# Delta rule of a two-block network: the triangular inverse transposed by VectorE in squares of 32

## The chip, the cores and the metric

The kernel runs on one core of a Trainium2 chip. The metric is the device time of one execution in microseconds (us); the time of the kernel before is the median of three runs.

## What is computed

The reference is a forward pass over 512 tokens of width 1024 (and 256 context tokens): a first block (dilated attention, a recurrent layer, a mixture of experts), and a second one of two layers (an even layer with attention and gated linear attention, an odd layer with a short convolution and a gated delta rule, each with an MLP). All of it is float32. The change touches the delta rule of the odd layer alone:

```python
def gdn_chunked(q, k, v, log_a, beta, s0):      # chunks of C = 64 tokens, 8 heads
    ...
    decay = jnp.where(incl, jnp.exp(jnp.where(incl, diff, 0.0)), 0.0)
    kb = k * beta
    a_mat = jnp.where(strict, jnp.einsum('bhnid,bhnjd->bhnij', kb, k) * decay, 0.0) + jnp.eye(C, dtype=F32)
    rhs = jnp.concatenate([v * beta, kb * jnp.exp(g)[..., None]], axis=-1)
    sol = lax.linalg.triangular_solve(a_mat, rhs, left_side=True, lower=True)
    ...
```

For every chunk and head a unit triangular matrix of 64x64 has to be inverted. It runs forwards and backwards over 768 tokens, which are 12 chunks.

## The kernel before

`delta` (line 3322) does the delta rule in a pipeline of STEPS = 12 problems. Problem `u` is one chunk forwards and one backwards (index z), for 8 heads each (the 8 heads lie as two halves of the 128 partitions, index g, and four columns of 64): sixteen matrices of 64x64, a tile of 128x512. Buffers and PSUM regions are there twice, for even and odd `u`.

The inverse is made by doubling. N is the strict triangle; six masks `lev[:, l]` (LEVELS = 6) cut out of it the blocks that join two finished blocks of 2^l to one of 2^(l+1). N0 is level 0. After level l the inverse so far is block-diagonal with blocks of 2^(l+1). It is kept transposed, in `Tt`. Level by level, from l = 1 to 5:

- `product(u, l)` (3458), TensorE: sixteen matmuls of 64x64x64, masked N times `Tt`, into PSUM region 0; then eight transposes of `Tt` through the identity (line 3471) into region 1.
- `take(u, l)` (3623), ScalarE: waits for both, copies region 0 to M and region 1 to T (lines 3627, 3628).
- `update(u, l)` (3474), TensorE: waits for both copies; sixteen matmuls T times M into region 0.
- `inverse(u, l)` (3744), VectorE: `Tt` minus region 0, into `Tt` (line 3753). For l = 5 also `Tb`, `Tt` times beta (line 3758).

Level 0 is `first(u)` (3449): sixteen matmuls of N0 with the identity, which is a transpose, and `inverse(u, 0)`, identity minus that, into `Tt` (line 3748). N itself comes from `sums`, `spread` and `keys` on TensorE, `differences` (3706) and `matrix` (3715: EB at line 3719, N at 3725, N0 at 3731) on VectorE, and `decays` (3630) with `eg` (3640) on ScalarE. The masked N of levels 1 to 5 are made by GpSimd in `level(u, l)` (3839, each operation has line 3824).

Each float32 matmul here is two instructions. A matmul reads one half of the partitions (rows 0 to 63 or 64 to 127) and writes one half of PSUM's partitions; which halves these are is in `rows(..., g)` and in the last argument of `piece`. `product` before reads half g and writes half z, bank g; `update` reads half z and writes half g, bank z.

The order of each engine's queue is written by hand, in a loop over n = 0 to 13 in which problem `new` = n goes through levels 0 to 2, `old` = n - 1 through levels 3 to 5 and `s` = n - 2 through the state recurrence (`values`, `minus`, `gain`, `from_state`, `outputs` on TensorE, `half` on VectorE and ScalarE, `fade` on ScalarE, `advance` and `collect` on VectorE). One pass of this loop is called a beat below. From u = 4 on (`lat`) a problem has outputs, and `spread`, `queries` and `scores` belong to it. TensorE's order in a beat is: product(old,3), sums, values, update(old,3), minus, keys, spread, product(old,4), first(new), gain, update(old,4), product(new,1), product(old,5), update(new,1), from_state, update(old,5), outputs, product(new,2), queries, weigh, update(new,2). VectorE's: differences, inverse(old,3), half, matrix(new), inverse(new,0), inverse(old,4), advance, inverse(new,1), inverse(old,5), collect, inverse(new,2), scores(old). ScalarE's: take(old,3), decays, half, take(old,4), fade, take(new,1), take(old,5), take(new,2), weights. `sums` waits for `scores` of the problem before the one before, which frees its PSUM region.

In the profile most matmuls have line 3408 (a helper) and are known by their tiles. The tiles N, N0, Tt, T, M and Tb lie in rooms that the profile calls gdn_raw and mlp_ring.

## Time and profile before

| | us |
|---|---|
| median of 3 runs | 2944.53 (2937.66 to 2946.17) |
| profiled execution | 2938.93 |
| span of its instructions | 2937.1 |
| mean granted TensorE clock | 0.965 |
| TensorE busy in the span | 2732.4 (93%) |
| VectorE busy | 1145.6 (39%) |
| ScalarE busy | 933.3 (32%) |
| GpSimd busy | 407.8 (14%) |

The table is over the whole network, of which the stage of the delta rule is a tenth: it starts with `sums` at 2215.74 us and gives its last outputs at about 2500 us. So the shares of the table say little about it, and the rows below are of this stage. Engines are PE (TensorE matmul), PEld (its weight loads), DVE (VectorE), ACT (ScalarE), POOL (GpSimd). In a timeline consecutive instructions of one form are merged: the first number is the start of the first, the second the time to the end of the last, and a bracket tells how long the engine had been idle and what released it.

### The profile page before, as it was taken

What the parts mean: (1) busy time and instruction counts of PE and PEld (TensorE: products, weight loads), DVE (VectorE), ACT (ScalarE), POOL (GpSimd) and SP (SyncE); (2) the same over time, 40 slices, a digit from 0 to 9 for tenths busy, and PEclk for the clock granted to TensorE, in tenths of its full rate; (3) what the DMA queues carried; (4) which work ended last, traced back from release to release, by engine and by line L of the source; (5) the groups of instructions that cost most, each with busy time, mean ns of one, the idle gap of its engine ahead of it and who ended that gap; (6) DMA issues with size and microseconds to landing.
All of it is one profiled execution on the core that took longest, in us unless ns stands there. A gap on an engine that the chain in (4) does not pass through costs nothing. (4 is left out here: it accounts for less than half of the span.)

```text
span 2937.1 us, 50199 instructions
## 1 busy us (share of the span) xinstructions
PE 2732.4 (93%) x21562; PEld 2054.4 (70%) x21562; DVE 1145.6 (39%) x1644; ACT 933.3 (32%) x1534; POOL 407.8 (14%) x334
## 2 busy tenths in 40 slices
PE   8988889999999899899999999998996788799998
PEld 6764654444444785666788888886785777688887
DVE  3225342322333416644432333323444454544333
ACT  4235331111112224355331221213474545432222
POOL 0005120000000402343100000010004564100001
PEclk9999889999999999999999999999998899899999
DMA  6537718999995212000112112111210000222331
GB/s 248 201 127 278 291 58 355 401 404 405 404 397 209 71 55 60 23 30 30 57 58 72 57 60 69 57 57 61 86 36 31 4 4 28 91 86 88 99 100 57
DMA packets 160240, 389.56 MB, mean 133 GB/s; under 512 B 16719, under 2 KB 107754, under 8 KB 147274
## 3 DMA queue, kind: packets, MB, share of 16 engines
q1 hardware_dynamic: 147834, 198.40, 20.0%
q10 hardware_dynamic: 12240, 188.75, 15.8%
q8 instruction: 129, 2.11, 0.3%
q14 instruction: 37, 0.30, 0.0%
HBM read 381.36 MB, written 5.77 MB: 132 GB/s over the span
## 5 line engine op out<-in xcount | busy, mean ns | idle before, releaser
L2143 PE MATMUL ps<-mlp_h_low,mlp_w_high 128*128 128x512 f32 (+1 forms) x768 | 272.0, 354 | 0.0
L2143 PE MATMUL ps<-mlp_h_high,mlp_w_high 128*128 128x512 f32 (+1 forms) x768 | 271.9, 354 | 0.0
L2143 PE MATMUL ps<-mlp_h_high,mlp_w_low 128*128 128x512 f32 (+1 forms) x768 | 271.6, 354 | 0.0
L1997 ACT ACTIVATE mlp_w_high<-mlp_ring 128x2048 fp32r<-128x2048 f32 x64 | 122.2, 1912 | 316.2 <-PE ps L2143 316.2
L2143 PE MATMUL ps<-mlp_x_low,mlp_w_high 128*128 128x512 f32 (+1 forms) x576 | 204.0, 354 | 0.0
L2143 PE MATMUL ps<-mlp_x_high,mlp_w_high 128*128 128x512 f32 (+1 forms) x576 | 203.9, 354 | 0.0
L2143 PE MATMUL ps<-mlp_x_high,mlp_w_low 128*128 128x512 f32 (+1 forms) x576 | 203.7, 354 | 0.0
L254 POOL TENSOR_TENSOR aT<-aT 128x512 f32<-128x512 f32 (+1 forms) x30 | 59.6, 1986 | 1031.1 <-ACT aT L246 1030.6
L2001 DVE TENSOR_TENSOR mlp_w_low<-mlp_ring,mlp_w_high 128x2048 fp32r<-128x2048 f32 x64 | 146.6, 2293 | 62.4 <-ACT mlp_w_high L1997 62.4
L2207 DVE SCALAR_TENSOR_TENSOR hT<-ps,mod,hT 128x512 f32<-128x512 f32 x96 | 63.5, 662 | 256.0 <-PE ps L2143 256.0
L2143 PEld LDWEIGHTS ps<-mlp_h_high,mlp_w_high 128*128 128x128 f32 x768 | 145.3, 189 | 20.4
L2143 PEld LDWEIGHTS ps<-mlp_h_high,mlp_w_low 128*128 128x128 f32 x768 | 145.1, 189 | 20.2
L2143 PEld LDWEIGHTS ps<-mlp_h_low,mlp_w_high 128*128 128x128 f32 x768 | 145.2, 189 | 20.0
L1863 DVE TENSOR_TENSOR hT<-hT,ps 128x512 f32<-128x512 f32 x128 | 79.4, 683 | 181.6 <-PE ps L1699 181.6
L2196 DVE TENSOR_TENSOR mlp_square<-mlp_relu 128x768 f32<-128x768 f32 (+1 forms) x64 | 52.8, 826 | 249.2 <-ACT mlp_relu L2165 248.8
L2165 ACT ACTIVATE mlp_relu<-ps 128x512 f32<-128x512 f32 x96 | 49.7, 527 | 296.2 <-PE ps L2143 218.4
L3171 PE MATMUL ps<-odd_x_high,conv_w_parts 128*128 128x512 f32 (+1 forms) x448 | 121.3, 358 | 3.1 <-DVE conv_w_parts L3269 3.1
L2143 PEld LDWEIGHTS ps<-mlp_x_high,mlp_w_high 128*128 128x128 f32 x576 | 108.9, 189 | 15.2
L2143 PEld LDWEIGHTS ps<-mlp_x_high,mlp_w_low 128*128 128x128 f32 x576 | 108.9, 189 | 15.3
L2143 PEld LDWEIGHTS ps<-mlp_x_low,mlp_w_high 128*128 128x128 f32 x576 | 108.9, 189 | 15.0
L1704 PE MATMUL ps<-e_wu,aT 128*64 128x512 f32 x512 | 116.9, 598 | 0.0
L1704 PE MATMUL ps<-e_wg,aT 128*64 128x512 f32 x512 | 116.2, 595 | 0.7 <-ACT aT L1784 0.7
(557 smaller groups left out, 5922.8 us busy)
## 6 DMA issues: line engine op xcount, KB each, us to landing
mlp_ring<-in_mlp_w_dram SPq DMA_DIRECT2D x64, 1024.0 KB, 5.3
e_wg<-in_w_gate_dram ACTq DMA_DIRECT2D x15, 4096.0 KB, 14.9
e_wu<-in_w_up_dram ACTq DMA_DIRECT2D x15, 4096.0 KB, 14.6
ring<-in_w_down_dram ACTq DMA_DIRECT2D x15, 4096.0 KB, 14.1
ring<-in_ada_w_dram SPq DMA_DIRECT2D x16, 2048.0 KB, 8.8
h_rest<-in_ada_w_dram SPq DMA_DIRECT2D x8, 2048.0 KB, 8.4
ring<-in_w_in_dram SPq DMA_DIRECT2D x6, 2048.0 KB, 11.1
proj_ring<-in_even_w_in_dram SPq DMA_DIRECT2D x8, 1024.0 KB, 5.0
```

Of the source, the lines that this page charges most:

```text
L254: pool.tensor_tensor(total, self.square_of(self.E, 0, self.T) if n == 1 else total, self.square_of(self.E, n, self.T), ALU.add)\
L1704: last = pe.matmul(E.ps[SLOTS * s:SLOTS * (s + 1), bank * BANK:(bank + 1) * BANK], xg[:, par, k, half * P + s * SLOTS:half * P + (s + 1) * ...
L1863: dve.tensor_tensor(E.hT[:, n, 0:S], E.hT[:, n, 0:S], E.bank(4 + n % 4), ALU.add).then_inc(added, 1)
L1997: act.activation(self.high[:, slot], self.ring[:, slot], ACT.Copy).then_inc(self.w_high, 1)
L2001: dve.tensor_tensor(self.low[:, slot], self.ring[:, slot], self.high[:, slot].bitcast(FP), ALU.subtract).then_inc(self.w_low, 1)
L2143: last = pe.matmul(bank(st, n, s, b - a), w[:, st % 2, k, n * P:(n + 1) * P], x[:, k, a:b], start=(k == 0 and p == 0), stop=(k == KT - 1 a ...
L2165: act.activation(r[:, n, a:b], bank(st, n, s, b - a), ACT.Relu).then_inc(relus, 1)
L2196: dve.tensor_tensor(sq[:, n, :], r[:, n, :], r[:, n, :], ALU.mult).then_inc(squares, 1)
L2207: dve.scalar_tensor_tensor(out=E.hT[:, k, a:b], in0=bank(st, n, s, b - a), scalar=E.mod[:, layer, 40 + k, s:s + 1], in1=E.hT[:, k, a:b], o ...
L3171: last = pe.matmul(E.bank(2 * (n % 3) + half, b - a), wp[:, part, n % 2, kk, :], xp[:, kk, a:b], start=(kk == 0 and i == 0), stop=(kk == K ...
```

## The change

- `product` loses its eight transposes. It reads half g and now writes half g, bank z.
- `update` reads half g and writes half g. T now has the layout of `Tt`, M the layout that the new `product` writes (`zi`).
- T is made by VectorE: `dve.transpose` turns every square of 32x32 of a 128x512 tile in its place, from SBUF to SBUF. The inverse so far has blocks of 32 at most where a T is needed, so this is its transpose. It stands right behind the subtraction of `inverse(u, l)` for l = 1 to 4.
- `first` is gone from TensorE. `inverse(u, 0)` subtracts N0 from the identity in SBUF, which gives T, and a transpose of it gives `Tt`.
- `take` copies M alone.
- `level(u, 3)` on GpSimd waits for the new T of level 0 in place of `first`.

Two names of semaphores that are no longer used are left out here:

```diff
--- before.py
+++ after.py
@@ -3352,6 +3352,7 @@
         azj = lambda t: t.rearrange("p (a z j n) -> p a z j n", a=2, z=2, j=2)
 
         iz = lambda t: t.rearrange("p (i z n) -> p z i n", i=4, z=2)
+        zi = lambda t: t.rearrange("p (z i n) -> p z i n", z=2, i=4)
         blocks = lambda t: t.rearrange("p (m n) -> p m n", n=64)
 
         def region(u, r):
@@ -3446,15 +3447,6 @@
                                     last = mm(piece(u, 1, a, 2 * z + j, g), rows(G.k, a)[:, ch, j, g], rows(G.q, a)[:, 2 * g + j, cols])
                     last.then_inc(kq[u % 2], 1)
 
-                def first(u):
-                    b = B[u % 2]
-                    pe.wait_ge(cst_in, 96)
-                    after(pe, n0, u)
-                    for i in range(8):
-                        for g in range(2):
-                            last = mm(piece(u, 0, i // 4, i % 4, g), rows(b["N0"], g)[:, 64 * i:64 * i + 64], rows(eye, g))
-                    last.then_inc(x[u % 2], 1)
-
                 def product(u, l):
 
                     b = B[u % 2]
@@ -3462,24 +3454,20 @@
                     after(pe, tt, u, l, 7)
                     n_, t_ = zaj(b[f"N{l % 3}"]), iz(b["Tt"])
                     for i in range(4):
-                        for g in range(2):
-                            for z in range(2):
-                                last = mm(piece(u, 0, g, i, z), rows(n_, g)[:, z, i // 2, i % 2], rows(t_, g)[:, z, i])
+                        for z in range(2):
+                            for g in range(2):
+                                last = mm(piece(u, 0, z, i, g), rows(n_, g)[:, z, i // 2, i % 2], rows(t_, g)[:, z, i])
                     last.then_inc(m[u % 2], 1)
-                    for i in range(4):
-                        for g in range(2):
-                            last = pe.transpose(pieces(u, 1, g, i), rows(b["Tt"], g)[:, P * i:P * i + P], rows(eye, g))
-                    last.then_inc(t[u % 2], 1)
 
                 def update(u, l):
                     b = B[u % 2]
                     after(pe, mc, u, l, 5)
-                    after(pe, tc, u, l, 5)
-                    t_, m_ = gaj(b["T"]), gaj(b["M"])
+                    after(pe, t, u, l, 5)
+                    t_, m_ = iz(b["T"]), zi(b["M"])
                     for i in range(4):
                         for z in range(2):
                             for g in range(2):
-                                last = mm(piece(u, 0, z, i, g), rows(t_, z)[:, g, i // 2, i % 2], rows(m_, z)[:, g, i // 2, i % 2])
+                                last = mm(piece(u, 0, z, i, g), rows(t_, g)[:, z, i], rows(m_, g)[:, z, i])
                     last.then_inc(x[u % 2], 1)
 
                 def weigh(u):
@@ -3576,8 +3564,6 @@
                             spread(new)
                     if old is not None:
                         product(old, 4)
-                    if new is not None:
-                        first(new)
                     if s is not None and s + 1 < STEPS:
                         gain(s)
                     if old is not None:
@@ -3623,9 +3609,7 @@
                 def take(u, l):
                     b = B[u % 2]
                     after(act, m, u, l, 5)
-                    after(act, t, u, l, 5)
                     act.activation(both(b["M"]), region(u, 0), ACT.Copy).then_inc(mc[u % 2], 1)
-                    act.activation(both(b["T"]), region(u, 1), ACT.Copy).then_inc(tc[u % 2], 1)
 
                 def decays(u):
                     b = B[u % 2]
@@ -3743,14 +3727,19 @@
 
                 def inverse(u, l):
                     b = B[u % 2]
-                    after(dve, x, u, l + 1, LEVELS)
                     if l == 0:
-                        dve.tensor_tensor(iz(b["Tt"]),
-                                          eye[:].unsqueeze(1).unsqueeze(1).to_broadcast([P, 2, 4, 64]),
-                                          region(u, 0).rearrange("p z (i n) -> p z i n", n=64), ALU.subtract).then_inc(tt[u % 2], 1)
+                        after(dve, n0, u)
+                        dve.tensor_tensor(iz(b["T"]), eye[:].unsqueeze(1).unsqueeze(1).to_broadcast([P, 2, 4, 64]), zi(b["N0"]),
+                                          ALU.subtract).then_inc(t[u % 2], 1)
+                        after(dve, t, u, 1, 5)
+                        dve.transpose(b["Tt"], b["T"]).then_inc(tt[u % 2], 1)
                     else:
+                        after(dve, x, u, l, 5)
                         after(dve, tt, u, l, 7)
                         dve.tensor_tensor(iz(b["Tt"]), iz(b["Tt"]), region(u, 0).rearrange("p z (i n) -> p z i n", n=64), ALU.subtract).then_inc(tt[u % 2], 1)
+                        if l < LEVELS - 1:
+                            after(dve, tt, u, l + 1, 7)
+                            dve.transpose(b["T"], b["Tt"]).then_inc(t[u % 2], 1)
                     if l == LEVELS - 1:
                         after(dve, tt, u, 6, 7)
                         if u >= 2:
@@ -3839,7 +3828,7 @@
                 def level(u, l):
                     after(pool, nn, u)
                     if l >= 3:
-                        after(pool, x if l == 3 else m, u, 1 if l == 3 else l - 3, LEVELS if l == 3 else 5)
+                        after(pool, t if l == 3 else m, u, 1 if l == 3 else l - 3, 5)
                     else:
                         after(pool, m, u - 2, l + 3, 5)
                     tt_(z4(B[u % 2][f"N{l % 3}"]), z4(B[u % 2]["N"]), mask(lev[:, l])).then_inc(nl[u % 2], 1)
```

## Rows read from the trace of the kernel before

**Rows 1.** Busy us (instructions) of PE, PEld, DVE, ACT, POOL in two beats; granted clock, DMA.

```profile
...
2215.74:2237.20 21.46, 11.64 (x256) 9.61 (x256) 5.99 (x8) 3.59 (x7) 7.74 (x6) 0.53 0.27 98
2361.40:2383.08 21.68, 18.47 (x668) 16.72 (x665) 11.53 (x16) 10.54 (x23) 13.11 (x13) 1.00 0.01 4
...
```

**Rows 2.** Grouped lines of the stage: count, busy us, mean ns, then idle time before.

```profile
...
L3753 DVE TENSOR_TENSOR mlp_ring<-mlp_ring,ps 128x512 f32<-128x512 f32 x60 | 41.3, 688 | 85.0 <-PE ps L3408 85.0
...
L3471 PE MATMUL ps<-gdn_eye,mlp_ring 64*128 64x64 f32 x480 | 29.1, 242 | 0.3 <-issue 0.3
...
L3408 PE MATMUL ps<-gdn_eye,gdn_raw 64*64 64x64 f32 x384 | 15.8, 239 | 20.4 <-DVE gdn_raw L3731 20.4
...
L3775 DVE TENSOR_TENSOR aT<-aT,ps 128x1024 f32<-128x1024 f32 x11 | 13.4, 1215 | 0.6 <-ACT aT L3655 0.6
...
```

**Rows 3.** Timeline, one steady beat, TensorE: start us, duration us, instruction.

```profile
...
2361.40 1.08 PE L3408 MATMUL ps<-gdn_LU,base 64*64 64x256 f32 x8
...
2362.32 1.80 PE L3408 MATMUL ps<-gdn_vt,mlp_ring 64*64 64x128 f32 x29
...
2363.96 0.67 PE L3408 MATMUL ps<-mlp_ring 64*64 64x64 f32 x27
...
2366.25 0.68 PE L3408 MATMUL ps<-mlp_ring,gdn_raw 64*64 64x64 f32 x32
...
2368.79 1.05 PE L3408 MATMUL ps<-gdn_eye,gdn_raw 64*64 64x64 f32 x29 [1.47 <-DVE gdn_raw L3731]
...
2371.08 0.66 PE L3408 MATMUL ps<-mlp_ring,gdn_raw 64*64 64x64 f32 x30
...
2382.07 0.69 PE L3408 MATMUL ps<-mlp_ring,gdn_raw 64*64 64x64 f32 x32 [0.88 <-DVE mlp_ring L3753]
...
2382.69 0.46 PE L3471 MATMUL ps<-gdn_eye,mlp_ring 64*128 64x64 f32 x8
...
2383.08 1.08 PE L3408 MATMUL ps<-gdn_LU,base 64*64 64x256 f32 x8
...
```

**Rows 4.** Timeline of the same beat, VectorE.

```profile
...
2364.77 0.69 DVE L3753 TENSOR_TENSOR mlp_ring<-mlp_ring,ps 128x512 f32<-128x512 f32 x1 [1.55 <-PE ps L3408]
...
2366.26 0.68 DVE L3719 TENSOR_TENSOR gdn_raw<-gdn_raw,gdn_BE 128x512 f32<-128x512 f32 x1
...
2367.23 0.69 DVE L3725 TENSOR_TENSOR gdn_raw<-gdn_raw,ps 128x512 f32<-128x512 f32 x1 [0.29 <-ACT gdn_eg L3640]
...
2367.95 0.69 DVE L3731 TENSOR_TENSOR gdn_raw<-gdn_raw,hT 128x512 f32<-128x512 f32 x1
...
2381.23 0.69 DVE L3753 TENSOR_TENSOR mlp_ring<-mlp_ring,ps 128x512 f32<-128x512 f32 x1 [1.74 <-PE ps L3408]
2381.84 0.68 DVE L3741 TENSOR_TENSOR gdn_qk<-gdn_EM,ps 128x512 f32<-128x512 f32 x1
...
```

**Rows 5.** Timeline of the same beat, ScalarE.

```profile
...
2366.55 0.60 ACT L3640 ACTIVATE gdn_eg<-ps 128x512 f32<-128x512 f32 x1 [2.00 <-PE ps L3408]
...
2379.12 0.60 ACT L3627 ACTIVATE mlp_ring<-ps 128x512 f32<-128x512 f32 x1 [4.07 <-PE ps L3471]
...
2379.61 0.59 ACT L3628 ACTIVATE mlp_ring<-ps 128x512 f32<-128x512 f32 x1
...
```

**Rows 6.** Timeline of the first beat, TensorE, granted clock 0.50.

```profile
...
2222.44 1.97 PE L3408 MATMUL ps<-gdn_eye,gdn_raw 64*64 64x64 f32 x32 [3.70 <-DVE gdn_raw L3731]
...
2228.38 1.13 PE L3408 MATMUL ps<-mlp_ring 64*64 64x64 f32 x32 [1.34 <-ACT mlp_ring L3628]
...
```

**Rows 7.** Timeline, GpSimd and VectorE beside each other, first and steady beat.

```profile
...
2220.48 2.94 POOL L3824 TENSOR_TENSOR gdn_raw<-gdn_raw,hT 128x512 f32<-128x512 f32 x2 [4.80 <-DVE gdn_raw L3725]
2220.51 1.78 DVE L3731 TENSOR_TENSOR gdn_raw<-gdn_raw,hT 128x512 f32<-128x512 f32 x1
...
2368.00 3.02 POOL L3824 TENSOR_TENSOR gdn_raw<-gdn_raw,hT 128x512 f32<-128x512 f32 x2 [7.99 <-DVE gdn_raw L3725]
...
```

**Rows 8.** Line 3758 (Tb), all twelve: min, median and max ns.

```profile
...
L3758 DVE TENSOR_TENSOR mlp_ring<-mlp_ring,gdn_BE x12: 692/1188/1673, 2250.6 to 2486.3; 128x512 f32<-128x512 f32 x12
...
```

More of the change, by code:

```diff
@@ L3368, in delta @@
         two = lambda n: [sem(f"delta_{n}{i}") for i in range(2)]
-        (lu, gj, gb, t1, ab_, eg, e, eb, em, kk, kq, nn, qk, nl, x, tt, m, t, mc, tc, w, wt, kg, ke, qd, n0) = (two(n) for n in (
-            "LU", "Gj", "gb", "t1", "abs", "eg", "E", "EB", "EM", "KK", "KQ", "N", "qk", "Nl", "X", "Tt", "M", "T", "M_out", "T_out",
+        (lu, gj, gb, t1, ab_, eg, e, eb, em, kk, kq, nn, qk, nl, x, tt, m, t, mc, w, wt, kg, ke, qd, n0) = (two(n) for n in (
+            "LU", "Gj", "gb", "t1", "abs", "eg", "E", "EB", "EM", "KK", "KQ", "N", "qk", "Nl", "X", "Tt", "M", "T", "M_out",
             "W", "W_out", "KG", "ke", "qd", "N0"))
```

## Prediction

> **What bounds the kernel now.** I read the busy times of the engines over two beats of the stage first [rows 1]. The change touches one stage, the delta rule, which runs from about 2215 to 2500 us of the span: twelve problems, a new one in each beat, each beat about 21 us long. In the beat from 2361.40 to 2383.08 us TensorE is busy 18.47 of 21.68 us at full clock (2.4 GHz), VectorE 11.53, ScalarE 10.54, GpSimd 13.11. TensorE has little slack, but it has some: the beat is a loop through TensorE and VectorE, and what counts is which wait ends last. The grouped lines of the stage [rows 2] give the sizes and counts: 60 updates of the inverse on VectorE of 0.69 us, 480 transposes on TensorE, 384 matmul instructions of `first`. Then I walked one beat on TensorE [rows 3], VectorE [rows 4] and ScalarE [rows 5]. The loop is this. `product(u,3)` starts (2382.07 is its start in the next beat); `sums` 1.01 later; `values` until about 2363.9; `update(old,3)`; VectorE's subtraction at 2364.77; EB, N and N0 on VectorE (2366.26, 2367.23, 2367.95); `first` at 2368.79, for which TensorE has been idle 1.47; `gain`, `update(old,4)`, `product(new,1)` at 2371.08, and from there TensorE goes nearly without a break to `update(new,2)`, behind which VectorE subtracts (2381.23) and the next beat's product starts 0.15 after its end.
>
> **What a block of 32 matmul instructions costs.** The rows show two rates. `product` now uses all four combinations of row half and output half: 32 instructions in 0.69, of which the last takes 0.22, so 0.47 / 31 = 15 ns each, a block of 0.48. `first` keeps rows and output on the same half: 29 in 1.05, (1.05 - 0.22) / 28 = 30 ns. `values`, the same kind with 128 columns, takes (1.80 - 0.27) / 28 = 55 ns, 27 for 64 columns. So a block of this kind is about 0.88 and its results are ready 1.15 after its start, against 0.69 [rows 3]. The new `product` and `update` are of that kind: they keep each problem on its half. At half clock (1.2 GHz) `first` lasts 1.97 and today's `update` 1.13 [rows 6].
>
> **The change, part by part, in a steady beat at full clock.**
> Removed from TensorE: `first` (0.88) and five sets of eight transposes. Product and transposes together hold TensorE 1.01 (2382.07 to 2383.08), the new product 0.90: 0.11 less, five times. Added: 0.40 in each of five updates. Net on TensorE: -0.9 - 0.55 + 2.0 = +0.55 us per beat. TensorE ends up with more work, not less.
> Removed from ScalarE: five copies of 0.59, each 0.49 behind the first [rows 5].
> Added to VectorE: five transposes of 128x512. No row shows one. The nearest rows are the operations of the same size, 0.69, or 0.72 from start to start where one waits for the other (2367.23 to 2367.95); I take 0.69. Ends: 0.35, half of that row, and 1.22, the row of the operation of twice the elements [rows 2]. VectorE goes from 11.5 to 15 of 22 us. The subtraction behind `first` stays at 0.69 but now reads two tensors from SBUF.
> The Trainium skill, VectorE: DVE Perf Modes, section "The three transpose paths", gives 311 ns for 128x128 bf16; scaled by element at 0.96 GHz an estimate by that page is 0.71 us. No row here shows it, and the sum doesn't use it.
>
> That subtraction has a price of its own. In the first beat a GpSimd operation with SBUF operands started at 2220.48 and N0 on VectorE 0.03 later; N0 took 1.78 in place of 0.69, the two GpSimd operations 2.94. In the steady beat N0 starts first, 0.05 ahead, keeps its 0.69, and the GpSimd pair takes 3.02 [rows 4, 7]. Tb, also with two SBUF operands, runs from 0.69 to 1.67 with GpSimd at work [rows 8]. Subtractions that read PSUM stay at 0.69 sixty times [rows 2]. So whichever of the two starts second waits for the other's whole operation. The new subtraction comes right behind N0, exactly when the GpSimd operation that was held by N0 goes ahead: it waits for that one ((3.02 - 0.49) / 2 = 1.26) and then ends 0.54 after it, as in the first beat. Cost 1.74 in place of 0.69; ends 0.69 and 1.78.
> The Trainium skill, SBUF — State Buffer, section "Who interferes with whom", states this as a rule: a VectorE instruction with two SBUF inputs and a GpSimd instruction that reads SBUF exclude each other for the whole instruction. The rows agree (0.69 against 1.78).
>
> Now the loop, each point as lateness against the beat of before, both counted from the start of `product(old,3)`:
> a. `sums` waits for `scores` of the problem before, which stands behind the last subtraction on VectorE. Today it starts 0.61 after that and is hidden (2381.84 to 2382.52, `sums` at 2383.08). With a transpose between them it ends 1.17 after the product starts and `sums` starts at 1.32 instead of 1.01: +0.31.
> b. `update(old,3)` ends 0.46 later: VectorE's subtraction at +0.77.
> c. Its transpose stands ahead of `half`, EB and N on VectorE. The subtraction starts at 2364.77 + 0.77 = 2365.54, the transpose 0.72 later, `half` 0.61 behind that (as two independent operations follow each other), EB 0.61, N 0.72: 2368.20, where N started at 2367.23 (it waited for ScalarE's `eg`, 2367.15, which is late by 0.71 only): +0.97.
> d. Today N0 at 2367.95 lets product(new,1) start at 2371.08. Now N0 at 2368.92; GpSimd's operation starts 0.05 later, is held 0.49 and ends at 2370.72; the subtraction ends 0.54 later at 2371.26, the transpose at 2371.98 and the product starts 0.15 after it, at 2372.13: 1.05, say +1.07 with the first instructions that the row leaves out. TensorE does `gain` and `update(old,4)` ahead of it and then stands idle: the idle time in front of `first` has moved, not gone.
> e. From here TensorE is the path. Three products are 0.11 shorter, two of them ahead of product(new,2); update(new,1) waits 0.19 for ScalarE; update(new,1) and update(old,5) are 0.40 longer. product(new,2) at 1.07 - 0.22 + 0.19 + 0.80 = +1.84.
> f. From product(new,2) to update(new,2): today 0.62 + 0.46 + 0.09 + 0.49 + 0.59 + 0.15 = 2.40 (product, transposes, two copies), now 1.15 + 0.09 + 0.60 + 0.15 = 1.99: -0.41. The update's result is 0.46 later: +0.46. Next beat: +1.89 us.
> The first beat runs at half clock with one problem alone (21.46 us): each of its two updates costs 0.84 more, its products with transposes lose about 0.3 each; the start through N0 wins 0.4: +0.7 in all. The other eleven: 11 x 1.89 = 20.8. TensorE also stalls inside blocks, about a microsecond per beat beyond what the blocks add up to; with 72 of some 670 instructions gone per beat (the 32 of `first`, 40 transposes), a tenth of that, and a little slack in front of product(new,1), I take 2.5 off for all beats. Sum: 0.7 + 20.8 - 2.5 = +19. The span is 2937.1, the profiled execution 2938.9, 5.6 under the median 2944.5 of the runs; on the median 2944.5 + 19 = 2963.5, say 2963.
>
> **The rivals.**
> 1. Faster: the new blocks run at today's 15 ns, because what makes `first` and `values` slow is something else than the same-half form. For it: nothing in the rows isolates the cause. Against it: `sums` is slow too (8 of 256 columns in 1.08, four times the columns at about 105 ns each), and these three share the form and little else. Then b falls away, two blocks in e and the one in f are 0.4 shorter, f gains another 0.46: the sum is about -0.4 per beat, 2939. The point from which it decides is a block of 0.67, halfway.
> 2. The subtraction isn't held up by GpSimd: d shrinks by 1.05, of which part is taken by TensorE, which then still has update(old,4) to finish: +0.8 per beat at most, +7 in all, 2951. For it: one of twelve N0 only was held. Against: Tb's median of 1.19 [rows 8].
> 3. The transpose costs 1.22, or waits for GpSimd like a two-operand operation: it stands in a, c and d, 0.5 each, so +1.6 more per beat: 2982.
> 4. The stalls inside TensorE's blocks shrink by half or more, since slower blocks ask for fewer instructions per microsecond: 0.5 to 1 less per beat, +8 to +13: about 2953.
> Another rule speaks against the change. The Trainium skill, TensorEngine Tiling (Array Packing), section "Gotcha 1: PSUM Pressure", says that different row tiles can't use one PSUM bank at once; new products write one bank from both row halves, the old ones didn't. `first` and `values` do that already and show 27 to 30 ns, so its price, if it is one, is in the sum.
>
> **How the numbers follow.** The forecast (1.2 to 2.6 us per beat, 2955 to 2974): 0.52. Rival 2: 0.15. Rival 3: 0.12. Rival 4: 0.12. Rival 1: 0.09. A difference of 0.3%, 8.8 us, is about what can be told from none. Slower by more: the forecast, rival 3, half of 2 and half of 4: 0.76. Faster by more: two thirds of rival 1 and a little of 4: 0.08. Within: 0.16. The range for 8 in 10 goes from 2946 (rival 2 whole, 4 nearly whole) to 2980 (half of rival 3), and leaves out rival 1.
>
> **What would show it.** Blocks of `product` and `update` with 27 to 30 ns per instruction; VectorE transposes near 0.69; the new two-operand subtraction near 1.7 in most beats; TensorE idle 1.5 to 2 us in front of product(new,1), no longer in front of `first`; `sums` held for `scores`; steady beats of 23.0 to 23.8 us where 21.7 stood; nothing changed outside the stage. I am wrong if the blocks take 15 ns, or if the subtraction keeps 0.69 and the beat stays below 22.3.

## The result, and the profile after

The changed kernel takes 2951.4 us, median of 7 runs (2946.8 to 2954.4), beside 2941.3 for the kernel before in the same session (2935.8 to 2946.2, 7 runs): a ratio of 1.0031, 95% interval 1.0018 to 1.0044. It is 10 us slower. The forecast was 18.5 slower, with a range that began 1.5 above the median of before that it started from. The sign holds, the time lies in the range, the size is about half. The profiled execution has a span of 2950.6 us where the one of before had 2937.1; the granted clock over the whole span is the same, 0.964 and 0.965.

First the beats, from the start of `sums` to the next, with each beat's granted clock. It is this table that the prediction should have made of the kernel before:

| beat | 1 | 2 | 3 | 4 | 5 | 6 | 7 | 8 | 9 | 10 | 11 | sum | to the out projection |
|---|---|---|---|---|---|---|---|---|---|---|---|---|---|
| before, us | 21.46 | 18.08 | 19.07 | 22.28 | 20.96 | 22.76 | 21.05 | 21.68 | 21.94 | 22.30 | 21.89 | 233.5 | 63.3 |
| clock | .53 | .89 | 1 | .83 | .91 | .88 | 1 | 1 | 1 | 1 | 1 | | |
| after, us | 22.05 | 20.20 | 20.49 | 20.50 | 20.61 | 21.80 | 23.69 | 23.71 | 24.05 | 23.70 | 23.73 | 244.5 | 59.8 |
| clock | .52 | .85 | 1 | 1 | 1 | 1 | .93 | .93 | .93 | .93 | .93 | | |

The last column runs from the twelfth `sums` to the first product behind the stage. The change is worth +11.1 in the eleven beats and -3.4 behind them, +7.6 in all. The other 5.9 of the 13.5 between the two spans is no work of the change: `sums` starts 6.7 us later in the trace of after (2222.47 against 2215.74), in code that is the same in both, and e1 below shows that this place wanders from one execution of a kernel to the next.

Windows of four stretches of the changed kernel (columns as in [rows 1]): the first beat, the fourth, a steady one, and 3 us inside the steady one.

```profile
...
2222.47:2244.52 22.05, 12.02 (x200) 10.38 (x202) 9.06 (x11) 2.62 (x5) 7.73 (x6) 0.52 0.26 95
2285.21:2305.71 20.50, 15.54 (x495) 14.95 (x492) 14.20 (x18) 7.77 (x17) 10.88 (x10) 1.00 0.01 4
2371.81:2395.52 23.71, 20.58 (x592) 19.83 (x593) 15.48 (x21) 8.14 (x19) 13.06 (x13) 0.93 0.01 3
2384.00:2387.00 3.00, 3.00 (x66) 3.00 (x67) 0.87 (x2) 0.78 (x2) 3.00 (x5) 0.50 0.03 5
...
```

The steady beat is 23.71 where [rows 1] had 21.68. TensorE is busy 20.58 in it against 18.47, with 592 instructions in place of 668; VectorE went from 11.53 to 15.48, ScalarE from 10.54 to 8.14. The fourth beat has less work on TensorE (495 instructions) and full clock.

The grouped lines of the stage: the updates that VectorE had, the copies that ScalarE keeps, and VectorE's new work.

```profile
...
L3739 DVE TENSOR_TENSOR mlp_ring<-mlp_ring,ps 128x512 f32<-128x512 f32 x60 | 40.6, 677 | 75.6 <-PE ps L3409 75.6
L3612 ACT ACTIVATE mlp_ring<-ps 128x512 f32<-128x512 f32 x60 | 35.9, 598 | 128.5 <-PE ps L3409 128.5
L3742 DVE STREAM_TRANSPOSE mlp_ring<-mlp_ring 128x512 f32<-128x512 f32 x48 | 34.1, 711 | 1.7
...
L3732 DVE TENSOR_TENSOR mlp_ring<-gdn_eye,gdn_raw 128x512 f32<-128x512 f32 x12 | 19.7, 1640 | 0.4
...
L3735 DVE STREAM_TRANSPOSE mlp_ring<-mlp_ring 128x512 f32<-128x512 f32 x12 | 8.5, 711 | 0.4
...
```

A transpose of 128x512 takes 711 ns, sixty times (48 at line 3742, 12 at 3735); the new two-operand subtraction 1640, twelve times. The 60 updates on VectorE are unchanged (677 against 688 in [rows 2]).

The timeline of one steady beat, TensorE's, VectorE's and GpSimd's rows that answer to [rows 3, 4, 7]:

```profile
...
2370.49 1.15 PE L3409 MATMUL ps<-mlp_ring,gdn_raw 64*64 64x64 f32 x32 [0.87 <-DVE mlp_ring L3739]
2371.02 0.65 DVE L3725 TENSOR_TENSOR gdn_qk<-gdn_EM,ps 128x512 f32<-128x512 f32 x1
...
2371.81 1.08 PE L3409 MATMUL ps<-gdn_LU,base 64*64 64x256 f32 x8 [0.17 <-DVE gdn_qk L3725]
...
2379.14 0.69 DVE L3715 TENSOR_TENSOR gdn_raw<-gdn_raw,hT 128x512 f32<-128x512 f32 x1
2379.18 3.46 POOL L3813 TENSOR_TENSOR gdn_raw<-gdn_raw,hT 128x512 f32<-128x512 f32 x2 [8.77 <-DVE gdn_raw L3709]
...
2379.46 1.11 PE L3409 MATMUL ps<-mlp_ring 64*64 64x64 f32 x32
2379.86 1.64 DVE L3732 TENSOR_TENSOR mlp_ring<-gdn_eye,gdn_raw 128x512 f32<-128x512 f32 x1
2381.54 0.71 DVE L3735 STREAM_TRANSPOSE mlp_ring<-mlp_ring 128x512 f32<-128x512 f32 x1
...
2382.40 2.66 PE L3409 MATMUL ps<-mlp_ring,gdn_raw 64*64 64x64 f32 x64 [1.83 <-DVE mlp_ring L3735]
...
2384.78 1.80 PE L3409 MATMUL ps<-mlp_ring 64*64 64x64 f32 x29
...
2394.20 1.15 PE L3409 MATMUL ps<-mlp_ring,gdn_raw 64*64 64x64 f32 x32 [0.87 <-DVE mlp_ring L3739]
...
```

`product(old,3)` lasts 1.15 for its 32 instructions (the first row). `scores` (line 3725) stands behind a transpose, and `sums` waits 0.17 for it. N0 on VectorE (line 3715) ends at 2379.83; the subtraction starts at 2379.86, beside a GpSimd pair that is held and that holds it, and takes 1.64; its transpose follows, and TensorE has stood idle 1.83 when `product(new,1)` starts at 2382.40. Then comes what the prediction did not have: the block of 64 instructions lasts 2.66, some 39 ns each, and the window from 2384 to 2387 has a granted clock of 0.50, half speed. It comes back at the same place in each of the beats 7 to 11.

### The profile page after: what moved, and what is told of

The parts are those of the page before. It is cut to its first block and busy times, and to the rows that moved or that the text cites. A ratio compares the mean times of both kernels' runs of the same rounds, so it can differ in the third digit from the quotient of the medians.

```text
span 2950.6 us, 48399 instructions
## 1 busy us (share of the span) xinstructions
PE 2745.6 (93%) x20698; PEld 2078.4 (70%) x20698; DVE 1193.8 (40%) x1704; ACT 904.0 (31%) x1474; POOL 411.0 (14%) x334
```

## Experiments

**e1 and e2: both kernels once more**, unchanged, on one chip.

> The kernel before, unchanged, profiled a second time. In its first profile TensorE's granted clock fell to half in parts of the beats that start at 2274, 2296 and 2317 us (means 0.83, 0.91, 0.88), and these beats took 22.3, 21.0 and 22.8 us where the like beat without it took 19.1; in the changed kernel the beats at the same place ran at full clock in 20.5, 20.6 and 21.8. Theory A (the half clock there belongs to the kernel before: its blocks and gaps bring it about each time): the spells are there again in the beats 3 to 5, and the stage from the first to the last sums takes 233 to 234 us again. Theory B (chance of the one profile): the spells lie elsewhere or are missing, and the stage takes 225 to 230 us.

> The changed kernel, unchanged, profiled a second time. Its stage took 244.5 us from the first to the last sums, 11.1 more than the kernel before. Theory A: 244 to 245 us again, at full clock in the beats 3 to 5. Theory B: half-clock spells fall into it somewhere in the stage, and it takes 247 to 253. Either way steady beats at full clock take 23.7 us and the two-operand subtraction 1.64 us.

Measured: 2939.2 and 2955.4 us, one run each. The kernel before had beats of 21.65, 20.48, 22.28, 22.00, 20.70, 21.44, 21.56, ... (clock .52, .75, .86, .84, .93, .92, then 1), in sum 236.0; after had 21.87, 20.52, 21.11, 20.50, 20.60, 21.80, 23.69, ... (clock .53, .84, .92, 1, 1, 1, then .93) in sum 245.2. With the stretch behind (62.0 and 61.4) the change is worth +8.7: -2.4 in beats 2 to 6, +11.4 in beats 7 to 11. `sums` starts at 2220.02 in e1, 4.3 later than in the first trace of the same kernel. So in the main the pattern belongs to each kernel: half clock in beats of the first half before, in beats of the second half after. Beat 3 is the exception in both: before it had 1.00 in the first trace and .86 in this one, after it had 1.00 and .92. Behind the stage the two traces of the kernel before differ by another 5 us, from the out projection to the end, without any change of code (424.6 and 419.4).

**e3: all four quarters again.** The new kernel with `product` and `update` fed from both halves, as they were; the numbers of the inverse are then others, the work is the same.

```diff
-            last = mm(piece(u, 0, z, i, g), ...)
+            last = mm(piece(u, 0, g, i, z), ...)
...
-            last = mm(piece(u, 0, z, i, g), rows(t_, g)[:, z, i], rows(m_, g)[:, z, i])
+            last = mm(piece(u, 0, z, i, g), rows(t_, z)[:, g, i], rows(m_, z)[:, g, i])
```

> The changed kernel with one thing undone: product and update read one half of the partitions and write the other as well, all four combinations, as in the kernel before; the VectorE transposes and all waits stay. It pairs the wrong halves, so the inverse isn't computed rightly; the number and size of the instructions is the same. Theory (the same-half form is the price): blocks of 32 take 0.69 us in place of 1.15, steady beats about 21.6 in place of 23.7 (2.1 less), the stage 22 to 27 us shorter than the changed kernel, so 10 to 15 us faster than the kernel before, about 0.995 of it. Rival (VectorE is the path; TensorE's longer blocks hide beside it): steady beats above 23 us, no more than 8 us gained.

Measured: 2925.5 us, ratio 0.9957 (0.9945 to 0.9969). Steady beats of 20.9 to 22.2 where after had 23.7:

```profile
...
2359.50:2380.44 20.94, 16.51 (x593) 15.71 (x593) 16.03 (x21) 8.01 (x19) 13.48 (x13) 0.92 0.01 4
...
```

TensorE is busy 16.51 in it for 593 instructions, against 20.58 for 592. The same-half form costs 2.8 us in this beat and 2.5 in the mean of the beats 7 to 11 (21.28 against 23.78), at nearly the same clock (0.92 and 0.93), and without it the rest of the change would be a gain of 0.4%.

**e4: the subtraction reads PSUM** in place of N0, so that VectorE has one SBUF operand; the block of PSUM is another, and so is the result.

```diff
-    dve.tensor_tensor(iz(b["T"]), eye..., zi(b["N0"]), ALU.subtract)
+    dve.tensor_tensor(iz(b["T"]), eye..., region(u, 0)..., ALU.mult)
```

> The changed kernel with the subtraction of level 0 replaced by an operation of the same size whose second operand is read from PSUM (identity times the product of the keys), so that it has one SBUF operand; the inverse isn't computed rightly. Theory (the 0.95 us are a wait for GpSimd on SBUF): the operation takes 0.69 in place of 1.64 beside the same GpSimd work, product(new,1) starts 0.95 earlier and steady beats take about 22.7 in place of 23.7; the stage is 10 to 12 us shorter, as long as the kernel before, ratio about 1.000. Rival (the form with a repeated operand is slow in itself): 1.64 stays whatever GpSimd does. Second rival (the gain is given back because TensorE is the path): 0.69, but beats above 23.3.

Measured: 2927.3 us, ratio 0.9965 (0.9948 to 0.9982). Timeline and window of its steady beat:

```profile
...
2360.62 3.01 POOL L3814 TENSOR_TENSOR gdn_raw<-gdn_raw,hT 128x512 f32<-128x512 f32 x2 [8.35 <-DVE gdn_raw L3709]
...
2361.31 0.69 DVE L3732 TENSOR_TENSOR mlp_ring<-gdn_eye,ps 128x512 f32<-128x512 f32 x1
...
2362.89 2.08 PE L3409 MATMUL ps<-mlp_ring,gdn_raw 64*64 64x64 f32 x64 [0.88 <-DVE mlp_ring L3736]
...
```

```profile
...
2353.26:2374.65 21.39, 19.21 (x593) 18.36 (x593) 15.53 (x21) 8.14 (x19) 13.04 (x13) 1.00 0.01 3
...
```

The subtraction takes 0.69 with the GpSimd pair at work beside it, TensorE is idle 0.88 in place of 1.83, and the beat is 21.39 instead of 23.7. The hold accounts for 0.95 of these 2.3 us, and only this part was expected. The other 1.4 is the clock: 1.00 in this beat, 64 instructions in 2.08 us where they took 2.66, and TensorE's busy time 1.37 shorter (19.21 against 20.58) for the same work.

**e5: the idle time filled.** Behind N0, TensorE runs 28 products of `ones` and `eye` into a region that is overwritten afterwards.

```diff
     if new is not None:
+        after(pe, n0, new)
+        warm(lambda i, g: piece(new, 1, i // 4 % 2, i % 4, g), 14)
         product(new, 1)
```

> The changed kernel with 28 matmuls of 64x64x64 more on TensorE (56 instructions, nobody reads them), put into the idle time of 1.83 us ahead of product(new,1), where TensorE waits for VectorE's transpose. In the changed kernel's steady beats the granted clock is at half for some 3.3 us after that idle time (blocks of 1.6 us in place of 0.9), and e4, where the idle time was 0.88, stayed at full clock and took 21.4 where 22.7 was expected. Theory (idle time brings the half clock, and that costs 1.3 of the 2.3 us): steady beats run at full clock and take 22.3 to 22.6 in place of 23.7, although TensorE does more work; 9 to 12 us less than the changed kernel, ratio to the kernel before about 0.999. Rival (the half clock has nothing to do with the idle time): clock 0.93 again and beats of 23.7 or more.

Measured: 2939.1 us, ratio 1.0004 (0.9989 to 1.0019) to the kernel before, so 0.3% under after. TensorE's timeline, and the window of the beat:

```profile
...
2370.76 1.81 PE L3409 MATMUL ps<-gdn_eye,base 64*64 64x64 f32 x56
2372.76 2.08 PE L3409 MATMUL ps<-mlp_ring,gdn_raw 64*64 64x64 f32 x64 [0.19 <-DVE mlp_ring L3742]
...
```

```profile
...
2362.18:2384.46 22.28, 20.79 (x648) 20.00 (x649) 15.82 (x21) 8.14 (x19) 13.50 (x13) 1.00 0.02 4
...
```

With 56 instructions more (648 against 592) the beats 7 to 11 take 22.39 in the mean, where they took 23.78, and the clock is 1.00 from the second beat on but for the sixth. The half-clock stretch cost about 1.4 us per beat, and in these beats it doesn't come without the idle time in front of it. In the sixth beat, which after had at full clock, it came at another place, behind 1.93 us of waiting for Tb. The filling also took the first beat from 21.9 to 19.0 (clock 0.73 for 0.52), which this experiment doesn't keep apart from the rest.

**e6: the same filling in the kernel before**, ahead of `first`.

```diff
+    if new is not None and s is not None:
+        ...
+        warm(lambda i, g: state(g, i % 4, i // 4 % 2, 1)[:, 0:64], 12)
     if new is not None:
         first(new)
```

> The kernel before with 24 matmuls of 64x64x64 more on TensorE (48 instructions, nobody reads them) in the idle time ahead of first, 1.5 to 1.7 us, from the beat of problem 2 on. Two profiles of the kernel before show half clock behind this idle time in the beats 2 to 5 (22.3, 22.0, 20.7, 21.4 where 19.1 to 20.4 is the beat without it), none later. Theory: these spells go and the beats 2 to 5 take 19.1 to 20.5; the stage from 233 to 236 goes to 226 to 229, ratio about 0.997. This would show that the kernel before paid for the half clock too, and why the change cost less than its steady beats. Rival: spells stay, ratio 1.000 or above.

Measured: 2945.3 us, ratio 1.0024 (1.0011 to 1.0037). It cost 7 us and freed none of the early beats of the low clock: beats 3 to 6 have .80, .91, .98 and .94, the last two a little more than in the two traces of before, and two later beats (.96, .97) now have less. TensorE's timeline, where the clock falls:

```profile
...
2265.38 1.05 PE L3408 MATMUL ps<-gdn_eye,gdn_raw 64*64 64x64 f32 x29 [0.50 <-DVE gdn_raw L3740]
...
2270.53 0.21 PE L3408 MATMUL ps<-mlp_ring,gdn_raw 64*64 64x64 f32 x1 [1.09 <-issue]
...
2272.46 0.69 PE L3408 MATMUL ps<-mlp_ring 64*64 64x64 f32 x32 [0.71 <-ACT mlp_ring L3637]
...
2274.69 1.13 PE L3408 MATMUL ps<-mlp_ring,gdn_KG 64*64 64x64 f32 x32
...
```

The idle time in front of `first` was down to 0.50, but the slow stretch (32 instructions of `weigh` in 1.13 from 2274.69 on; at full clock it is 0.65) now comes behind two other gaps, 1.09 under "issue" and 0.71 behind ScalarE. So this doesn't settle whether the kernel before would run faster at full clock.

**e7: the kernel before with same-half blocks**, nothing else (again with other numbers in the inverse).

```diff
-                last = mm(piece(u, 0, g, i, z), ...)
+                last = mm(piece(u, 0, z, i, g), ...)
...
-                last = mm(..., rows(t_, z)[:, g, i // 2, i % 2], rows(m_, z)[:, g, i // 2, i % 2])
+                last = mm(..., rows(t_, g)[:, z, i // 2, i % 2], rows(m_, g)[:, z, i // 2, i % 2])
```

> The kernel before with one part of the change alone: product and update read and write the same half; PE transposes, first and both copies stay. The halves that update pairs are no longer the right ones, so the inverse isn't computed rightly; instructions are the same in number and size. Theory (a block of 32 costs 0.40 to 0.46 more and TensorE is the path): ten blocks per beat, 3 to 3.6 us more per steady beat (24.7 to 25.5 at full clock), 35 to 45 us in all, ratio 1.012 to 1.016. If the stalls inside TensorE's blocks (about 1.3 us per beat in the kernel before, none seen in the changed one) come from the pace of the short blocks, they vanish here too and the sum is 23.9 per steady beat, 22 to 30 us in all, ratio 1.008 to 1.010. Rival (blocks hide beside VectorE): less than 1 us per beat, ratio below 1.004.

Measured: 2959.1 us, ratio 1.0076 (1.0050 to 1.0102). TensorE's timeline and the window of a steady beat:

```profile
...
2379.70 1.10 PE L3408 MATMUL ps<-mlp_ring,gdn_raw 64*64 64x64 f32 x32
...
2384.02 1.13 PE L3408 MATMUL ps<-mlp_ring 64*64 64x64 f32 x32
2384.95 1.13 PE L3408 MATMUL ps<-mlp_ring,gdn_raw 64*64 64x64 f32 x32
...
```

```profile
...
2374.33:2398.72 24.39, 22.28 (x668) 20.89 (x665) 11.19 (x16) 10.67 (x23) 12.65 (x13) 1.00 0.01 3
...
```

24.39 with the same 668 instructions as [rows 1]: +2.7, and full clock in every beat from the third on. Ten blocks with 0.40 more each are +4.0. Part of the difference is waiting that the longer blocks cover: the idle time ahead of `first` is 1.0 where it was 1.47. The larger part is that the kernel before stalls inside its blocks, and after and e7 don't. TensorE's waits of the kernel before from 2338 us on (us in total, times, longest):

```profile
...
PE ps L3408 <- DVE gdn_raw L3731: 8.5, 6, 1.5
...
PE ps L3408 <- issue: 4.6, 9, 1.0
...
```

And two of these stalls in the beat of [rows 3]:

```profile
...
2372.17 0.57 PE L3408 MATMUL ps<-mlp_ring,gdn_raw 64*64 64x64 f32 x22
2373.03 0.44 PE L3408 MATMUL ps<-mlp_ring,gdn_raw 64*64 64x64 f32 x10 [0.29 <-issue]
...
2375.68 0.87 PE L3408 MATMUL ps<-gdn_vn,gdn_qk 64*64 64x128 f32 x12
2376.85 1.19 PE L3408 MATMUL ps<-gdn_vn,gdn_qk 64*64 64x128 f32 x17 [0.30 <-issue]
...
```

The profile lists 0.29 and 0.30. Counted from when the next instruction was due, 22 instructions at 15 ns and 12 at 55 ns after the start of their rows, they are 0.53 and 0.51. With the 0.14 that the last update is longer than 0.69 this beat holds 1.2 us of them. That the pace of the blocks alone decides this isn't shown: e3 has the fast form, but fewer instructions, and under "issue" only 0.9 us in five beats.

**e8: the transposes queued later.** Each stands in VectorE's queue behind the work that another engine waits for.

```diff
-    if l < LEVELS - 1:
-        after(dve, tt, u, l + 1, 7)
-        dve.transpose(b["T"], b["Tt"]).then_inc(t[u % 2], 1)
...
+def turn(u, l):
+    after(dve, tt, u, l + 1, 7)
+    dve.transpose(B[u % 2]["T"], B[u % 2]["Tt"]).then_inc(t[u % 2], 1)
...
     matrix(new)
+    turn(old, 3)
     inverse(new, 0)
```

> The changed kernel with VectorE's queue in another order, everything computed: the transpose of level 3 goes behind N0, where VectorE otherwise waits for GpSimd, that of level 4 behind advance, that of level 1 behind the subtraction of level 1 as before, that of level 2 behind scores. Theory: half, EB and N are no longer held up (0.7 us), the subtraction's wait for GpSimd shrinks to 0.5 since a transpose runs in it, sums doesn't wait for scores, and TensorE is idle for less than 1.2 us at a time, so at full clock: steady beats 21.6 to 21.9 in place of 23.7, early ones 20.3; stage 225 to 228 us, ratio to the kernel before 0.996 to 0.999. Rival (TensorE's longer blocks are the path and nothing moves): beats of 23 and more, ratio above 1.001.

Measured: 2933.5 us, ratio 0.9985 (0.9971 to 0.9998). The steady beat, and its subtraction:

```profile
...
2361.94:2383.36 21.42, 19.01 (x599) 18.16 (x596) 15.27 (x22) 8.14 (x18) 13.48 (x13) 1.00 0.01 3
...
```

```profile
...
2391.57 1.13 DVE L3732 TENSOR_TENSOR mlp_ring<-gdn_eye,gdn_raw 128x512 f32<-128x512 f32 x1
...
```

21.42 at full clock in place of 23.7. The places of the transposes in the queue are worth 2.3 us per beat here: points a and c of the prediction, a shorter hold (1.13), and the clock.

**e9: GpSimd behind the subtraction.** One wait more on GpSimd.

```diff
     after(pool, nn, u)
+    if l == 1:
+        after(pool, t, u, 1, 5)
```

> The changed kernel with one wait more: GpSimd's mask of level 1 waits for the subtraction of level 0 and so starts behind it; everything is computed. Theory (the hold by GpSimd costs 0.95, and a further 1.3 through the half clock behind the idle time): the subtraction takes 0.69 in place of 1.64; GpSimd's level 1 then ends about 1.3 us behind it, 0.5 later than the transpose that took over, so product(new,1) starts 0.4 to 0.5 earlier, the idle time falls from 1.83 to about 1.4, and if the clock stays up steady beats take 21.8 to 22.1 in place of 23.7, ratio about 0.998 to 1.000. If the idle time is still long enough for the half clock: 23.2, ratio 1.002. Rival (no hold): nothing changes or it gets slower by the later mask, ratio 1.004.

Measured: 2937.2 us, ratio 0.9984 (0.9974 to 0.9994). The subtraction keeps 691 to 693 ns; now TensorE waits for GpSimd, in the usual beat and in one with a longer wait:

```profile
...
2372.69 2.08 PE L3409 MATMUL ps<-mlp_ring,gdn_raw 64*64 64x64 f32 x64 [1.44 <-POOL gdn_raw L3813]
...
2394.82 2.08 PE L3409 MATMUL ps<-mlp_ring,gdn_raw 64*64 64x64 f32 x64 [1.80 <-POOL gdn_raw L3813]
...
```

```profile
...
2395.00:2400.00 5.00, 5.00 (x170) 5.00 (x170) 3.23 (x5) 1.20 (x2) 5.00 (x8) 1.00 0.02 3
...
```

The usual beat is 21.8 at full clock, with an idle time of 1.44; the one with 1.80 took 22.1, also at full clock. In the beats 7 to 11 of after 1.82 to 2.18 went with half clock every time. The difference between 1.80 and 1.83 is small, so the length of this one gap hardly decides the clock by itself. The trace of after says the same more strongly. TensorE's rows in its beats 4 and 5:

```profile
...
2295.66 2.08 PE L3409 MATMUL ps<-mlp_ring,gdn_raw 64*64 64x64 f32 x64 [2.52 <-DVE mlp_ring L3735]
...
2316.28 2.08 PE L3409 MATMUL ps<-mlp_ring,gdn_raw 64*64 64x64 f32 x64 [1.83 <-DVE mlp_ring L3735]
...
```

The same idle time at the same place, as long or longer (2.52 and 1.83), and the block behind it runs at full clock, 2.08 for 64.

**e10: only the removal of `first`.** The kernel before, with the subtraction from N0 and one transpose for `first`; the other transposes and copies stay on TensorE and ScalarE.

```diff
-    first(new)
...
+    dve.tensor_tensor(iz(b["T"]), eye..., b["N0"]..., ALU.subtract).then_inc(x[u % 2], 1)
+    after(dve, x, u, 1, LEVELS)
+    dve.transpose(b["Tt"], b["T"]).then_inc(tt[u % 2], 1)
```

> The kernel before with the other part of the change alone: first is gone from TensorE; VectorE subtracts N0 from the identity in SBUF and transposes the result, product and update keep all four combinations of halves, PE transposes and both copies stay; everything is computed. Theory: the subtraction is held by GpSimd (1.6 us), which with the transpose takes as long as first and its subtraction did; TensorE loses 0.9 us of work but becomes idle for 2.3 us or more ahead of product(new,1), so the half clock comes in every beat; the stalls in the short blocks stay. Steady beats 21.5 to 23, ratio 0.999 to 1.004. Rival (taking first off TensorE, the path, is worth its 0.9 us per beat): beats of 20.8, ratio 0.996.

Measured: 2938.3 us, ratio 0.9989 (0.9977 to 1.0001), not told apart from none. The subtraction takes 1644 ns and the transpose 711 here too, and TensorE is idle 1.77 in front of `product(new,1)`:

```profile
...
2390.86 0.69 PE L3408 MATMUL ps<-mlp_ring,gdn_raw 64*64 64x64 f32 x32 [1.77 <-DVE mlp_ring L3740]
...
```

The beats are 21.1 to 22.3, clock 1 in most and .92 in some. This part of the change is about neutral; the loss is in the rest.

**e11 and e12: the best of it.** e11 is e8 with the filling of e5 in the first beat alone; e12 is the kernel before with the same filling.

```diff
+    if new == 0:
+        after(pe, n0, new)
+        warm(lambda i, g: piece(new, 1, i // 4 % 2, i % 4, g), 14)
```

> e8 (VectorE's transposes later in its queue) with 28 matmuls that nobody reads ahead of product(0,1) in the first beat, where TensorE is otherwise idle for 3.6 us and more and then runs at half clock for the whole beat; everything is computed. In e5 the same filling brought full clock from the middle of the first beat and 19.0 us in place of 21.9. Theory: the first beat takes 19.0 in place of 21.9, the rest stays as in e8 (20.1 early, 21.4 steady), stage 226 to 228 us, ratio to the kernel before 0.996 to 0.998, and faster than both kernels. Rival (the clock there follows something from before the stage): first beat 21.9 or, as the filling is work at half clock, 22 and more, ratio 0.998 to 1.000.

> The control to e11: the kernel before with the same 28 matmuls that nobody reads in its first beat, ahead of first, where TensorE is idle for 3.7 us. e11 was 0.9955 of the kernel before, e8 without the filling 0.9985; the difference of 0.3% is the filling. If the filling gives the kernel before the same (first beat 18 to 19 us in place of 21.5, full clock from its middle on), its ratio is 0.997 to 0.999 and the change with its queue reordered is worth only about 0.15 to 0.3% by itself; rival: here the filling is over before the next idle time, the clock stays at half, first beat 21.5, ratio 1.000, and e11's whole lead belongs to the changed kernel.

Measured: e11 2927.2 us, ratio 0.9955 (0.9939 to 0.9971), 0.45% under the kernel before and some 0.75% under after, with everything computed. Of the 0.3% by which it is ahead of e8, some 9 us, the traces show 3.5 in the stage (226.5 against 229.95 from the first to the last `sums`); where the rest lies isn't shown. e12 2943.7, ratio 0.9999 (0.9986 to 1.0011). The first beat of e11 and a later one:

```profile
...
2213.56:2232.67 19.11, 11.56 (x256) 10.23 (x258) 9.08 (x11) 2.62 (x5) 7.75 (x6) 0.73 0.31 110
2353.95:2375.38 21.43, 19.02 (x599) 18.17 (x597) 15.27 (x22) 8.14 (x18) 13.48 (x13) 1.00 0.01 4
...
```

The first beat went from 21.9 to 19.1 (clock 0.73). In e12 it is 21.65, as it was:

```profile
...
2229.54 1.97 PE L3408 MATMUL ps<-gdn_eye,gdn_raw 64*64 64x64 f32 x32 [1.81 <-DVE gdn_raw L3738]
...
```

`first` still starts behind 1.81 us of idle time, at half clock (1.97 for 32, as in [rows 6]). So the filling is no gain in itself. In e11 it lies directly ahead of the work, which fits; but the two kernels differ in more than that, and in e6 a filling directly ahead of `first` gained nothing.

## Why the prediction was right in sign and wrong in size

**The blocks (right).** 1.15 for 32 instructions, against 0.69. e7 and e3 show from both sides that the same-half form is the cause: rival 1 falls. The Trainium skill, TensorEngine Tiling (Array Packing), "Gotcha 1: PSUM Pressure", would have two row tiles unable to share a PSUM bank at once; the new products write one bank from both row halves and run at 28 to 30 ns, about the rate of `first`. Whether that rate is this rule's price or comes from using only two of the four combinations of halves wasn't tried.

**The transposes (right).** 0.711 against 0.69 taken; the upper end of 1.22 and rival 3 fall. The estimate from the Trainium skill, VectorE: DVE Perf Modes, "The three transpose paths", was 0.71, and the trace agrees.

**The hold by GpSimd (right).** 1.64 against 1.74, in all twelve; e4 and e9 give 0.69 without it. Rival 2 falls. The rule of the Trainium skill, SBUF — State Buffer, "Who interferes with whom", agrees with all three.

**The loop, points a to d (right).** From the start of `product(old,3)`, `sums` was forecast at 1.32 and is at 1.32 (2371.81 - 2370.49). `product(new,1)` was forecast at 10.64 + 1.07 = 11.71 and is at 11.91. (The 10.64 counts from a start 1.01 ahead of `sums`, as in the next beat; in the beat that was read `product(old,3)` itself had stalled and started at 2360.10, 0.29 earlier.) The idle time in front of it is 1.83 (1.5 to 2 forecast). Steady beats of 23.0 to 23.8 were forecast; they are 23.7, and 24.05 once.

**Points e and f (right in sum, by two mistakes that cancel).** The steady beat was to rise by 1.89 less some 0.2 for stalls, and rose by 2.0 (mean of beats 7 to 11, 23.78 against 21.77). But the stalls inside the blocks went wholly, 1.2 us in the beat that was read where 0.2 was taken, which is rival 4 in mechanism; and the half clock behind the moved idle time costs 1.4 (e4, e5), which no step of the prediction had. Rival 4 was right and hidden, and that the steady beat came out as forecast is luck.

**The sum over the beats (wrong, and the cause of the miss).** The step that failed is "The other eleven: 11 x 1.89 = 20.8". It took one steady beat's price for all, and with it a kernel before that runs all of them at full clock. In place of 20.8, less the 2.5 for stalls, the eleven measured 7.0 in the first pair of traces and 8.5 in the second. Place by place:

| | forecast | measured |
|---|---|---|
| beat 1 | +0.7 | +0.6 |
| beats 2 and 3 | +3.8 | +3.5 |
| beats 4 to 6 | +5.7 | -3.1 |
| beats 7 to 11 | +9.4 | +10.0 |
| the last, up to the out projection | +1.9 | -3.4 |
| stalls, for all | -2.5 | (in the beats) |
| sum | +19.0 | +7.6 |

Beats 4 to 6 came out 8.8 under their line and the end 5.3; the line for stalls gives 2.5 of this back. The second pair of runs (e1, e2) puts it a little elsewhere, with the same sign: +9.4 was forecast for beats 2 to 6, and they measure +0.5 in the first pair and -2.4 in the second; the end is -3.4 and -0.6; beats 7 to 11 are +10.0 and +11.4. In the early beats the kernel before doesn't run at full clock. Its windows of beats 4 to 6, and 4.5 us inside the first of them:

```profile
...
2274.35:2296.63 22.28, 17.40 (x565) 15.86 (x561) 10.29 (x13) 10.21 (x22) 10.03 (x10) 0.83 0.02 4
2296.63:2317.59 20.96, 16.70 (x570) 14.70 (x568) 9.88 (x13) 10.58 (x23) 11.68 (x11) 0.91 0.01 3
2317.59:2340.35 22.76, 18.05 (x603) 16.05 (x601) 10.26 (x14) 10.57 (x23) 13.08 (x13) 0.88 0.02 4
2281.50:2286.00 4.50, 4.47 (x128) 4.46 (x128) 1.01 (x2) 1.85 (x7) 4.50 (x7) 0.62 0.02 5
...
```

And how it begins, TensorE's row ahead of that stretch:

```profile
...
2281.53 1.43 PE L3408 MATMUL ps<-gdn_eye,gdn_raw 64*64 64x64 f32 x29 [1.69 <-DVE gdn_raw L3731]
...
```

`first`, behind 1.69 us of idle time, takes 1.43 for 29 instructions where [rows 3] have 1.05, and the clock of the next microseconds is 0.62. After the change these beats have full clock (1.00 in the table), though they too have an idle time of 1.83 to 2.52; why it costs nothing there isn't shown. What this costs the kernel before shows in its own beat 3, which has full clock in the first trace and not in e1 (the first trace, then e1):

```profile
...
2255.28:2274.35 19.07, 14.64 (x565) 13.19 (x561) 9.87 (x13) 10.21 (x22) 10.46 (x10) 1.00 0.01 3
...
2262.15:2284.43 22.28, 17.40 (x563) 15.54 (x561) 10.31 (x13) 10.15 (x22) 10.04 (x10) 0.86 0.02 4
...
```

The same work takes 3.2 us more, 2.8 of them in TensorE's busy time. Where both kernels have full clock, in beat 3 of the first traces, the change costs 1.4 (20.49 against 19.07), near the 1.7 that the prediction has for a beat with its share of the stalls. Beat 4 has the same work: after takes 20.50, and the kernel before 22.28 at .83. So there the change would cost 1.4 at equal clock and gains 1.8.

What full clock would have given the kernel before in the beats 4 to 6 can be estimated from e7, which has it in all of them: its beats 4 to 6 take 66.9, less 3 x 2.6 for its blocks makes 59.1, where before took 66.0. Seen so, the change costs 62.9 - 59.1 = 3.8 there, of the sign and nearly the size that was forecast, and gets back 7 from the clock. That is an estimate from rows: neither e6 nor e12 freed the kernel before of its low clock, so the 7 us were never measured as a whole. The stretch behind the last `sums` is another matter. In the first pair the clock of its working part is .92 and .94 before and 1.00 after, and the change is worth -3.4; in the second pair both have .92 and then 1.00, and it is -0.6. So some 2.8 of the 3.4 go with the clock of one execution, and the +1.9 that was forecast for this stretch isn't there at equal clock either. Why is open: no run looked at it.

**What stays open.** Why an idle time brings half clock at one place and not at another: 1.83 does in the beats 7 to 11 of after, 2.52 and 1.83 don't in its beats 4 and 5; 1.69 does in beat 4 of before, 1.47 doesn't; 1.77 (e10) sometimes does, 1.80 (e9) and 0.88 (e4) don't. Even the same gap in the same kernel goes both ways: ahead of `first` in beat 3 of before it is 1.70 in both traces, and in beat 3 of after, ahead of `product(new,1)`, it is 2.53 in both. In the first trace after had lost the clock behind the second beat only where TensorE has the most to do, but e2 lost it in beat 3 too, and no run changed that alone.

## What to carry to other kernels

Before a price per beat is multiplied, list every beat with its time and its granted clock; the two beats that were read hid that three others ran at another clock. A change that moves an idle time on TensorE can move the place where the clock falls, so both belong in the range: what the new place may lose and what the old one may get back. And when an engine gets new work, its place in the queue counts as much as its duration: the same sixty transposes are 0.3% slower than before in one order and 0.15% faster in another.

## What the runs showed of the hardware that was not expected

Idle times of TensorE of 1.7 to 1.8 us inside an otherwise busy stretch were in some beats followed by some 3 us at 1.2 GHz (0.50 granted from 2384 to 2387), and in others not, even at the same place of the same kernel (beat 3 of before, 1.00 and .86). Filling such a gap with products that nobody needs gave back 1.4 us per beat (e5), though it did nothing for the kernel before (e6, e12).

The short instructions of the kernel before, which pair row halves and output halves in all four ways, didn't keep their 15 ns: it lost 1.2 us in a steady beat to stalls inside blocks, which the profile lists under "issue" (0.3 to 1.0 each), and e7 and after, with 28 to 30 ns each, show none in their steady beats. So half the rate cost 2.7 us per beat and not 4.0.

A VectorE transpose of 128x512 in fp32 was 711 to 715 ns in all sixty, also beside GpSimd, while the subtraction in front of twelve of them, with two SBUF inputs, took 1.64. So the operation with one SBUF input wasn't held here.
